# One step of a hybrid decoder on one core: the second half of the up projection, pairs 1 to 8, as seven block products for eight

## The reference, cut to what matters

```python
n2 = rmsnorm(h, ln2)
up = n2 @ w_up                       # 544 x 1024 @ 1024 x 5632, float32
u, vv = up[..., :D_FF], up[..., D_FF:]
uc, conv_tail = causal_dwconv(u, conv_prev, conv_w, conv_b)   # width 3
h = h + (jax.nn.gelu(uc, approximate=False) * vv) @ w_down    # D_FF = 2816
```

## Time and profile before

| | us |
|---|---|
| median of 3 executions (844.35 to 847.52) | 845.63 |
| the profiled execution | 844.77 |
| its span, first to last instruction | 842.8 |
| busy in it: PE (matmul) / PE weight load | 830.2 / 818.9 |
| busy in it: DVE / ACT / POOL | 536.6 / 375.6 / 182.7 |
| DMA, mean over the span | 153 GB/s |
| granted TensorE clock, mean | 0.995 |

### The profile page before, as it was taken

One profiled execution on the slowest core, in us unless ns is written; L12 is line 12 of the kernel. 1 busy time (PEld: TensorE's weight loads), 2 busy tenths in 40 slices (PEclk: granted clock), 3 DMA queues, 4 the chain that ended last, 5 costly groups with the idle time before them and its releaser, 6 DMA issues.

```text
span 842.8 us, 16289 instructions
## 1 busy us (share of the span) xinstructions
PE 830.2 (99%) x6634; PEld 818.9 (97%) x6634; DVE 536.6 (64%) x671; ACT 375.6 (45%) x479; POOL 182.7 (22%) x224
## 2 busy tenths in 40 slices
PE   9999999999999999999999999999999999999996
PEld 8999999999999999999999999999999999999996
DVE  4464678486899776766565554544544555878973
ACT  5553244332445453544244534443443344644574
POOL 3017246343324200000400412222212122000020
PEclk9999999999999999999999999999999999999998
DMA  8769988982327992534892762133123323655522
GB/s 263 215 201 175 277 247 183 229 273 92 118 79 132 194 244 95 184 128 151 225 220 80 158 179 92 57 100 100 53 97 100 100 75 99 213 173 172 172 70 106
DMA packets 138527, 128.94 MB, mean 153 GB/s; under 512 B 5494, under 2 KB 130122, under 8 KB 138461
## 3 DMA queue, kind: packets, MB, share of 16 engines
q1 hardware_dynamic: 106636, 97.15, 37.2%
q0 software_dynamic: 31680, 30.55, 20.2%
q10 hardware_dynamic: 160, 0.53, 0.2%
HBM read 122.24 MB, written 41.62 MB: 194 GB/s over the span
## 4 chain that ended last, share of the span: by engine, by line
PE 91%; DVE 5%; ACT 1%; issue 1%; DMA 1%; DVEq 0%; SPq 0%; ACTq 0%
PE mm L1844 62%; PE mm L2235 8%; PE ax L2235 6%; PE ax L1863 6%; PE mm L2135 3%; PE ax L2135 3%; PE ax L1868 2%; DVE grs L1308 1%; DVE wlo L1298 1%; DMA raw<-in_w_in 1%; PE mm L1856 0%; DVE s0g L1465 0%; DVE wlo L1555 0%; ACT whi L907 0%; DVE ylo L1543 0%
## 5 line engine op out<-in xcount | busy, mean ns | idle before, releaser
L1844 PE MATMUL mm<-nhi,whi 128*128 128x272 f32 x1216 | 256.1, 292 | 1.2 <-DVE wlo L1343 0.6
L1844 PE MATMUL mm<-nhi,wlo 128*128 128x272 f32 x1216 | 252.3, 289 | 0.0
L1844 PE MATMUL mm<-nlo,whi 128*128 128x272 f32 x1216 | 251.4, 288 | 0.0
L1844 PEld LDWEIGHTS mm<-nhi,whi 128*128 128x128 f32 x1216 | 192.2, 189 | 3.8 <-DVE wlo L1298 0.8
L1844 PEld LDWEIGHTS mm<-nlo,whi 128*128 128x128 f32 x1216 | 191.6, 189 | 0.0
L1844 PEld LDWEIGHTS mm<-nhi,wlo 128*128 128x128 f32 x1216 | 190.7, 190 | 0.0
L907 ACT ACTIVATE whi<-raw 128x2048 fp32r<-128x2048 f32 (+2 forms) x79 | 114.4, 1466 | 94.8 <-PE mm L1844 69.3
L1298 DVE TENSOR_TENSOR wlo<-raw,whi 128x2048 fp32r<-128x2048 f32 x44 | 103.7, 2356 | 28.7 <-ACT whi L907 28.6
L907 ACT ACTIVATE whi<-ring 128x1408 fp32r<-128x1408 f32 x25 | 34.6, 1383 | 44.1 <-PE ax L2235 24.0
L907 ACT ACT_TABLE_LOAD x22 | 28.2, 1283 | 58.3 <-DVE ext L1683 56.7
L2235 PE MATMUL mm<-bhi,whi 128*128 128x272 f32 x176 | 51.4, 292 | 0.0
(11 more groups left out here) (351 smaller groups left out, 1557.1 us busy)
## 6 DMA issues: line engine op xcount, KB each, us to landing
raw<-in_w_up SPq DMA_DIRECT2D x44, 512.0 KB, 4.4
raw<-in_w_in SPq DMA_DIRECT2D x36, 512.0 KB, 5.2
ring<-w_sums SPq DMA_DIRECT2D x16, 704.0 KB, 4.1
w_sums<-in_w_down SPq DMA_DIRECT2D x12, 704.0 KB, 11.4
w_sums<-in_w_down POOLq DMA_DIRECT2D x12, 704.0 KB, 16.8
ring<-in_w_down SPq DMA_DIRECT2D x9, 704.0 KB, 4.6
w_sums<-w_sums POOLq DMA_DIRECT2D x8, 704.0 KB, 9.6
g_sums<-in_w_in SPq DMA_DIRECT2D x18, 256.0 KB, 5.5
```

The costliest lines, as they stand in the source:

```text
L1844: ins = pe.matmul(mm[:, 2 * j + a, 0:HALF], w, x[:, kx, HALF * a:HALF * (a + 1)], start=first and n == 0 and m == 0, stop=last and n == le ...
```

## The change

1. The v units of pairs 1 to 8 become "four" and "three" in the scheme of the gate stage, on the banks of `ax`. Pairs 0, 9 and 10 stay. The list `UPS` has all units of the stage: u and v, or u, four, three.
2. The pair's end on DVE changes: instead of two products out of PSUM there are five half adds and two full products, the second with a factor -1. ACT copies products 1, 2 and 3 away.
3. The sums of the activations n for this stage (`usum`, `uhigh`, `ulow`) are made in pair 0 and pair 1.
4. The weight sums of v (`v_sums`, 8 units x 4 sums of 256 KB) take the places of down's: begun by SP's copies in the head, two completed by POOL after the head, one copied from another there and completed together with the fourth when the output projection begins. "Four" of pair 1 waits for three of the sums, "three" for the fourth.
5. Down's sums are begun by SP beside the output projection and the first four pairs, and completed by POOL behind the pairs: two DMAs after most of them (one after pairs 1 and 2, four copies after pair 5).
6. SP's loop over the output projection's loads and the loops over the up projection on all five engines are written out; PE's loop over `w_o` stays.
7. In the gate stage the fourth low part of the sums (`t_low(3)`) goes behind the split of the next unit.
8. A block product from the sixth block on waits for the block before it, not for the second before it: successive blocks now use the same banks.

```diff
+UPS = []
+for _i in range(KF // 2):
+    UPS += [("u", _i)] + ([("four", _i), ("three", _i)] if 1 <= _i <= 8 else [("v", _i)])
+U_DOWN = U_UP + len(UPS)
+UP_BLOCKS = range(1, 9)
...
+    TB = R + KF * T + 2 * BB
+    HB = HALF * 4
+    usum, ulow = ([[(at(f"{n}{i}", [P, 4, HALF], TB + 4 * i * HB, dt), 4)] for i in range(4)]
+                  for n, dt in (("usum", F32), ("ulow", F32R)))
+    uhigh = [[(at("uhigh0", [P, 4, HALF], TB + 16 * HB, F32R), 4)],
+             [(at("uhigh1", [P, 4, HALF], R + 18 * T, F32R), 4)], [(at("uhigh2", [P, 4, HALF], R + 20 * T, F32R), 4)],
+             [(at("uhigh3", [P, 2, HALF], TB + 20 * HB, F32R), 2),
+              (at("uhigh3b", [P, 2, HALF], R + KF * T + BB + 9 * HB, F32R), 2)]]
+    u_sum = at("u_sum", [P, HALF], R + KF * T + 9 * HB)
+    v_sums = nc.dram_tensor("v_sums", [P, len(UP_BLOCKS), 4, 4 * P], F32).ap()
...
-    FD = [n + KF for n in FU]
+    FD = [n + KF - len(UP_BLOCKS) for n in FU]
...
+    PIECED = [u for u in range(U_BLOCK, U_DOWN) if u < U_WO or gate_kind(u) in ("four", "three")
+              or gate_kind(u) and gate_kind(u - 2) == "four"]
...
+    def up_fills(j, i):
+
+        return FU[j] + 2 * i - min(max(i - 1, 0), len(UP_BLOCKS))
+
+    def up_block(i):
+
+        return 6 + i - 1
...
-        begun = [(i, m) for i in (S_1, S_3, S_4) for m in range(MD)]
+        begun = [(i, m) for i in (S_3, S_1, S_4) for m in range(MD)]
+
+        def begin_sums(n):
+            for i, m in begun[2 * n:2 * n + 2]:
+                sp.dma_start(w_sums[i, :, m], w_block(*{S_1: (0, 1), S_3: (0, 0), S_4: (1, 0)}[i], m)).then_inc(sum_begun[i], 16)
...
-            for i, m in begun[2 * (u - 9):2 * (u - 8)] if u >= 9 else ():
-                sp.dma_start(w_sums[i, :, m], w_block(*{S_1: (0, 1), S_3: (0, 0), S_4: (1, 0)}[i], m)).then_inc(sum_begun[i], 16)
+            if u >= 9:
+                i, block = gs_copies[(u - 9) // 2]
+                for n in range(1 + 4 * ((u - 9) % 2), 5 + 4 * ((u - 9) % 2)):
+                    sp.dma_start(v_sum(i, n), v_block(*block, n)).then_inc(vs_begun[i], 16)
...
+        for n in range(4):
+            load((U_WO + n) % 2, U_WO + n - 1, *cols(w_o, UC * n))
+            if n % 2 == 1:
+                begin_sums(n // 2)
+        for n, (kind, i) in enumerate(UPS):
+            u = U_UP + n
+            if kind in ("u", "v"):
...
+                if i == 1:
+                    for k in (G_1, G_2, G_3) if kind == "four" else (G_4,):
+                        sp.wait_ge(vs_done[k], 16 * len(UP_BLOCKS))
+                block_load(u, kind, w_up, D_FF + UC * i, v_sums[:, i - 1])
...
+            if kind == "u" and i < 4:
+                begin_sums(2 + i)
...
+        def v_weight_sum(n, begun, added):
+
+            pool.wait_ge(vs_begun[n], begun)
+            for i in UP_BLOCKS:
+                pool.dma_start(v_sum(n, i), added(i), accum_op=ALU.add).then_inc(vs_done[n], 16)
+
+        all_sums = 16 * len(UP_BLOCKS)
+        v_weight_sum(G_3, all_sums, lambda i: v_block(0, 1, i))
+        v_weight_sum(G_1, all_sums, lambda i: v_block(1, 1, i))
+        pool.wait_ge(vs_done[G_3], all_sums)
+        for h in (slice(0, 4), slice(4, 8)):
+            pool.dma_start(v_sums[:, h, G_2], v_sums[:, h, G_3]).then_inc(vs_begun[G_2], 16)
+        pool.wait_ge(m_lo, KD)
+        v_weight_sum(G_2, 32, lambda i: v_block(1, 1, i))
+        pool.wait_ge(vs_done[G_2], all_sums)
+        v_weight_sum(G_4, all_sums, lambda i: v_sum(G_2, i))
...
+        for i in range(KF // 2):
             up_pair(i)
+            if i < 3:
+                weight_sum(S_3, ((0, 1), (2,), (3,))[i], (0, 1))
+            elif i < 5:
+                weight_sum(S_1, ((0, 1), (2, 3))[i - 3], (1, 1))
+            elif i == 5:
+                pool.wait_ge(sum_done[S_3], 16 * MD)
+                for m in range(MD):
+                    pool.dma_start(w_sums[S_2, :, m], w_sums[S_3, :, m]).then_inc(sum_begun[S_2], 16)
+            elif i < 8:
+                weight_sum(S_2, ((0, 1), (2, 3))[i - 6], (1, 1))
+            elif i < 10:
+                pool.wait_ge(sum_done[S_2], 16 * MD)
+                weight_sum(S_4, ((0, 1), (2, 3))[i - 8], S_2)
...
+        for k in range(4):
+            run(tile(usum[0], k), resid[:, k, HALVES[1]], ACT.Copy, t_first, scale=vec(V_LN2 + k))
+        for i in range(KF // 2):
+            x, b = up_unit(i), up_block(i)
             for j in range(2):
                 t = i * 2 + j
-                act.wait_ge(drained[j], i * 2 + FU[j] + 1)
+                if j == 1 and i in UP_BLOCKS:
+                    keep(gact[:, 2 * i, HALVES[0]], ax, b, 0)
...
+                    next_hi(x)
+                if j == 1 and i in UP_BLOCKS:
+                    keep(gact[:, 2 * i + 1, HALVES[1]], ax, b, 1)
                 act.wait_ge(conv_done, t + 2)
-                act.wait_ge(drained[j], i * 2 + FU[j])
+                if i > 0:
+                    act.wait_ge(*gact_made(j, i - 1))
                 st.did(act.activation(gl[j][:, 0:SEQ], cb[:, 0:SEQ], ACT.Gelu))
                 run(gl[j][:, SEQ:NT].rearrange("p (b t) -> p b t", t=DEC_SEQ), conv_seqs, ACT.Gelu, gelu_done)
-            act.wait_ge(drained[0], i * 2 + FU[0] + 2)
-            run(bhi[0][:, bass.ds(i, 1), :], gact[:, bass.ds(i, 1), HALVES[1]], ACT.Copy, b_hi)
-            u = U_UP + 1
-            hi(u + 2, u % 2, i * 32 + 32 * (u // 2 + 2), (filled[1], i * 2 + FU[1] + 2))
-        st.n += 2 * (KF // 2 - 1)
+                if i == 1 and j == 0:
+                    t_high(usum, uhigh, 3)
+            if i in UP_BLOCKS:
+                act.wait_ge(block_added, 4 * b)
+                keep(u_sum[:, :], ax, b, 2)
+                next_hi(x + 1)
+            act.wait_ge(*gact_made(0, i))
+            run(bhi[0][:, i, :], gact[:, i, HALVES[1]], ACT.Copy, b_hi)
+            next_hi(x + (2 if i in UP_BLOCKS else 1))
+            if i == 0:
+                t_high(usum, uhigh, 0)
+                t_high(usum, uhigh, 1)
+                t_high(usum, uhigh, 2)
...
-                        t_low(2 + j)
+                    if q == 0 and j == 0:
+                        t_low(tsum, tlow, thigh, 2)
                 next_lo(u)
+                if q == 0:
+                    t_low(tsum, tlow, thigh, 3)
...
+                if i == 0 and j == 0:
+                    make_sums(usum, V_LN2, 0)
+                if i == 1 and j == 0:
+                    t_low(usum, ulow, uhigh, 1)
+                    t_low(usum, ulow, uhigh, 2)
+            next_lo(x)
+            if blocked:
+                dve.wait_ge(block_kept, 3 * b + 3)
+                st.did(dve.tensor_tensor(out[1][:, HALVES[1]], out[1][:, HALVES[1]], u_sum[:, :], ALU.add))
+                st.wait()
+                dve.wait_ge(block_done, 7 * b + 4)
+                dve.tensor_tensor(out[1][:, HALVES[1]], block(0, 3), out[1][:, HALVES[1]], ALU.add).then_inc(block_added, 1)
+                if i == 1:
+                    t_low(usum, ulow, uhigh, 3)
+                dve.wait_ge(block_done, 7 * b + 5)
+                dve.tensor_tensor(out[0][:, HALVES[1]], block(0, 1), u_sum[:, :], ALU.add).then_inc(block_added, 1)
+                next_lo(x + 1)
+                dve.wait_ge(block_done, 7 * b + 6)
+                dve.tensor_tensor(out[0][:, HALVES[0]], block(0, 2), out[0][:, HALVES[0]], ALU.add).then_inc(block_added, 1)
             for j in range(2):
...
+                elif j == 0:
+                    dve.wait_ge(block_added, 4 * b + 3)
+                    dve.tensor_tensor(out[0], out[0], gl[0][:, :], ALU.mult).then_inc(block_scaled, 1)
+                else:
+                    dve.wait_ge(block_done, 7 * b + 7)
+                    dve.tensor_tensor(out[1][:, HALVES[0]], block(0, 3), u_sum[:, :], ALU.add).then_inc(block_added, 1)
+                    dve.wait_ge(block_added, 4 * b + 4)
+                    dve.scalar_tensor_tensor(out[1], out[1], -1.0, gl[1][:, :], op0=ALU.mult, op1=ALU.mult
+                                             ).then_inc(block_scaled, 1)
...
+                if i == 0 and j == 0:
+                    make_sums(usum, V_LN2, 1)
+                    make_sums(usum, V_LN2, 2)
+            next_lo(x + (2 if blocked else 1))
+            if i == 0:
+                make_sums(usum, V_LN2, 3)
+                t_low(usum, ulow, uhigh, 0)
...
+            last = b - 2 if b < 6 else b - 1
+            if start and last >= 0:
+                pe.wait_ge(block_kept, 3 * last + 3)
+                if product:
+                    pe.wait_ge(block_added, 4 * last + {1: 2, 3: 4, 5: 3}[product])
...
+        for n, (kind, i) in enumerate(UPS):
+            u = U_UP + n
+            if kind in ("u", "v"):
                 for j in range(2):
-                    pe.wait_ge(drained[j], i * 2 + (FU[j] + n))
-                    product(j, u % 2, j, every, nhi, nlo, ready=ready if first and n == 0 and j == 0 else None
-                            ).then_inc(filled[j], 1)
-
-        up(0, first=True)
-        with pe.Fori(1, KF // 2) as i:
```

(17 more changed lines are left out.)

325 lines of the change are left out of this document (163 added, 162 removed).

## The result

The changed kernel took **836.05 us** (median of 4 executions, 835.47 to 837.84) and the kernel before 846.30 (4 executions) beside it: a ratio of **0.9885**, 95% interval 0.9859 to 0.9911. On a second occasion it was 836.50 (5) against 845.61 (9), 0.9888 [0.9872, 0.9904]. Forecast were 837.5 us, and faster. The profiled execution took 837.84 us for a span of 836.0.

A forecast was written before the change was run, and what follows sets the result against it. PE was taken to bound the kernel, fully busy in the up projection. -12.04 - 0.7 + 4.7 = -8.0 us gave 836.7 profiled, 837.5 us as median; own range 835.4 to 839.5, 8-in-10 range 832.5 to 843.0.

The forecast's parts named there:

- 96 matmuls, -12.04 us: Up projection: eight pairs use 84 matmuls where a v unit took 96, saving 96 x 0.1254 = 12.04 us on PE.
- Pairs 2 to 8 without a wait: Up projection: added DVE, ACT and POOL work costs PE 0 in these pairs; bounds 0 and 0.5 us a pair.
- The fifth product's margin: Blocked pair, first product of "three": weight split ready at 17.4, wanted at 18.06 less 0.2 to 0.4; about 0.3 us spare.
- Pair 1, 4.7 us: First blocked pair: building the sums of n delays PE, costing 4.7 us; bounds 2.6 and 6.
- its three parts: Pair 1 losses: third product 2.6 us (copy), fifth 1.55 (weight split), seventh 0.55 (fourth low part).
- Gate stage, -0.7 us: Gate stage: fourth low part behind the split removes PE's 0.74 us wait for m_kept; gain 0.7, bounds 0 and -0.74.
- Transfers, no cost: v sums in down's old places and down's additions two behind a pair: POOL and loads stay in time, 0 us.
- The sum: Whole kernel: -12.04 - 0.7 + 4.7 = -8.0 us.
- the one without a stall in pair 1: Rival, pair 1: high parts overlap with the sum groups, so 12.7 us comes back, 832.9 us; chance 0.12.
- A small stall in each pair: Rival, fifth product: 0.5 us for each of seven further pairs gives 841.0 us, up to 843; chance 0.15.
- the late load: Rival, up projection: load of "four" lands late beside POOL's additions, costing 22 us, 859.5 us; chance 0.07.

The follow-up runs named there:

- the run without blocks: Changed kernel with all eleven v units computed the plain way, everything around them kept: 844.31 us against 845.03 for the kernel before, ratio 0.9983.
- the run with the repeated split: Changed kernel with the first piece of the low part of "three" computed once more in pairs 2 to 5, twice more in 6 to 8: 855.05 us.
- the two edits that remove it: Changed kernel with the sums of n moved into DVE's gaps (832.35 us), plus POOL's first multiplication in pair 1 waiting for the split of "three": 830.65 us, 0.9825.
- with the additions first: Version with both edits, with down's additions of a pair issued by POOL before its two multiplications of gl instead of after: 856.89 us.

## Why the prediction was right

*96 matmuls, -12.04 us*: right, and 0.26 too large, since a matmul of a block product takes 0.1256 us here and a plain one 0.1253. The blocked pairs take 22.58 to 22.61 us, and the run without blocks gives the rest of the change no effect on PE in this stage.

*Pairs 2 to 8 without a wait*: right, with 16.9 of 22.6 us of DVE busy where I had 17. The fifth product's margin was under-sized (0.3; measured about 0.7): in pair 2 the split's first piece ends at 514.84, 17.1 us after 497.74 and not 17.4, and the product starts at 515.67. From a piece to its product PE needs 0.1 us, as the run with the repeated split shows, where I had allowed 0.2 to 0.4.

*Pair 1, 4.7 us*: measured 4.6 by starts, but its three parts were off and cancelled; that the sum fits this well is luck. The third product lost 1.50 (2.6 forecast: DVE reached the second and third low part at 484.50, 0.8 us sooner), the fifth 1.68 (1.55), the seventh 1.40 (0.55). The last is the step that I did not see: I gave the add of u_sum 0.44 us from the gate stage, where POOL is idle (0.00 busy in its window), and in up it takes 1.62. That pair 1's loss is only an order of work is shown by the two edits that remove it.

*Gate stage, -0.7 us*: too small (-1.19, outside my bounds of 0 and -0.74), and I named one cause where the runs show two. I named only the low part that was put behind the split; undone in the changed kernel it costs 0.23, at the fifth product, a place that I had not looked at. The wait for m_kept goes by the lighter traffic alone, as the kernel before shows when its own additions are taken away. Whether the order alone would have removed it under the old traffic, as I forecast, no run tests. I had also read the wait from its row: 0.74, where starts give 0.97 (310.21 to 311.24, less a pitch, and a slow matmul behind). The row counts from the modelled end of a matmul, 0.29 after its start, while the pitch is 0.125.

*Transfers, no cost*: right in the result and too sure in its argument. The DMA share in up rose from 0.32 to about 0.8 and no load makes PE wait. But in pair 5 the load goes out only 0.75 us ahead of four copies; the one time that it went out behind them it took 13.4 us. No run moves that order alone.

*The sum*: -8.0 forecast, -8.26 by starts if the second dip of the clock is left out, -6.8 with it, and -10.2 and -9.1 in medians. *Rivals*: the one without a stall in pair 1 did not come, though two moves of code bring it about. A small stall in each pair and the late load did not come either, and the runs show both a small step away.

## What to carry to other kernels

When a form of work is copied from one stage to another, its durations do not come along: ask which engine is busy beside it in the new place, and above all whether POOL computes while DVE has two operands in SBUF. Read what a stall costs from the starts of matmuls and not from the wait's row alone, and put the one-time preparation of a new form into gaps that the timeline shows before counting its price as fixed. When large transfers of two issuers run beside each other, the moment of issue can matter as much as the bytes: write down who is issued first, and by how much.

## What the runs showed of the hardware

DVE and POOL took turns, one whole instruction at a time. A DVE add with both operands in SBUF took 0.43 us alone and 1.62 with POOL's multiplication running; POOL's took 1.36 alone and 2.11 with a split running. The Trainium skill says so (SBUF — State Buffer, SBUF: two separate sides): the port pair that DVE and GpSimd share is an exclusive lock, and a DVE operation with two SBUF inputs contends for it against a GpSimd operation that reads SBUF. The trace agrees, by the eight adds at 434 ns once POOL waits; I had not looked for it.

A transfer of 768 KB took 4.4 to 6.4 us when it was issued ahead of POOL's additions or copies, 6.3 to 9.6 behind one or two additions (in the runs with the split repeated and with the additions first), 13.4 behind four copies of 704 KB issued 1.6 us earlier, and 17.3 with four additions in flight and SP's issue held for 7.4 us. The last two were seen once each.

In the up projection PE's clock fell to the lower of its two levels during or behind every wait of 2.4 us and more (eight of 2.4 to 11.0 us in three runs, and one of 15.5 us in the kernel before with its additions late), and behind none of 1.6 us and less. Behind a wait of 2.9 us it stayed there for some 3.4 us (granted 0.57 over 4 us), at a price of 1.3 us that no row of waits shows.
